# Which engine makes the second half of the weights' low parts in a two-block transformer kernel

## The reference, cut to what matters

```python
# block 1
h = rms_norm(x, norm_g)
dq, dk, dv, dg, mq, mk, mv, mg, gates = split(h @ w_in)
o_a = diff_attention(rope(dq), rope(dk), dv, lam) * silu(dg)     # 4 heads of 2 maps
o_b = moba_attention(rope(mq), rope(mk), mv) * silu(mg)          # 8 heads
merged = sigmoid(g_a) * (o_a @ w_branch_diff) + sigmoid(g_b) * (o_b @ w_branch_moba)
x = x + merged @ w_out            # then a gate: x + sigmoid(x @ w_ple_gate) * (p @ w_ple), final norm
# block 2
mod = silu(c) @ w_mod + b_mod     # six rows of 1024: shift, scale, gate, twice
h = rmsnorm(x) * (1 + sc1) + sh1
q, kc, vc, ks, vs, kw, vw, gates, cb, cc, ch = split(h @ w_in_2)
mixed = [norm(sparse_attention(...)), norm(cb * causal_conv(cc * ch))]
x = x + gt1 * (mixed @ w_out_2)
h2 = rmsnorm(x) * (1 + sc2) + sh2
q = h2 @ peer_wq                  # 16 experts of 128*128 per head and token by these keys
x = x + gt2 * sum_e gelu(h2 . u_e) * g_e * v_e                   # over all 16384 rows of u and v
```

## Time and profile before

| what | value |
|---|---|
| median of 3 runs | 1235.44 us (1234.71 to 1236.09) |
| the profiled execution's own time | 1233.38 us |
| its span, first to last instruction | 1231.6 us |
| busy in the span | PE 1191.4, DVE 910.5, ACT 782.5, POOL 565.2 us |
| PE clock granted, mean | 0.996 of full speed |

### The profile page before, as it was taken

One profiled execution on the slowest core, in us unless ns is written; L12 is line 12 of the kernel. 1 busy time (PEld: TensorE's weight loads), 2 busy tenths in 40 slices (PEclk: granted clock), 3 DMA queues, 4 the chain that ended last, 5 costly groups with the idle time before them and its releaser, 6 DMA issues.

```text
span 1231.6 us, 26652 instructions
## 1 busy us (share of the span) xinstructions
PE 1191.4 (97%) x8256; PEld 1070.6 (87%) x8256; DVE 910.5 (74%) x1885; ACT 782.5 (64%) x1784; POOL 565.2 (46%) x505
## 2 busy tenths in 40 slices
PE   8999999989998999999999999999999999999997
PEld 8888988988877999888999999998888888888886
DVE  5777768888577839996788888761676767686766
ACT  5446676465765555667877888876656555555555
POOL 3664543445464358998877777778100000000000
PEclk9999999999999999999999999999999999999999
DMA  6668655538643445655666666667676676767663
GB/s 233 227 212 296 235 193 202 172 121 290 249 140 120 137 138 179 185 185 170 214 212 197 204 213 201 210 209 266 203 245 212 189 258 189 260 197 257 191 196 108
DMA packets 85828, 249.86 MB, mean 203 GB/s; under 512 B 8019, under 2 KB 29692, under 8 KB 84988
## 3 DMA queue, kind: packets, MB, share of 16 engines
q1 hardware_dynamic: 77356, 209.62, 53.7%
q0 software_dynamic: 8400, 39.34, 8.7%
HBM read 237.38 MB, written 13.12 MB: 203 GB/s over the span
## 4 chain that ended last, share of the span: by engine, by line
PE 84%; DVE 6%; ACT 4%; issue 3%; POOL 3%; DVEq 0%; POOLq 0%; ACTq 0%
PE psum L695 83%; POOL w_lo L1645 2%; ACT w_hi L1218 1%; DVE w_lo L1815 1%; DVE s_sb L1829 1%; PE psum L896 1%; DVE arena L1868 1%; DVE rstd L1809 0%; ACT arena L1377 0%; ACT arena L1201 0%; DVE arena L2024 0%; DVE xres L1949 0%; DVE arena L1930 0%; ACT L1377 0%; DVE arena L2074 0%
## 5 line engine op out<-in xcount | busy, mean ns | idle before, releaser
L695 PE MATMUL psum<-h_parts,w_hi 128*128 128x256 f32 (+1 forms) x3216 | 676.3, 303 | 17.0 <-DVE h_parts L1859 4.4
L1645 POOL TENSOR_TENSOR w_lo<-ring,w_hi 128x512 fp32r<-128x512 f32 x368 | 490.7, 1344 | 273.3 <-ACT w_hi L1218 264.6
L1218 ACT ACTIVATE w_hi<-ring 128x512 fp32r<-128x512 f32 x734 | 445.2, 628 | 254.2 <-PE psum L695 243.7
L695 PEld LDWEIGHTS psum<-h_parts,w_hi 128*128 128x128 f32 x3216 | 515.5, 191 | 53.4 <-issue 21.2
L695 PE MATMUL psum<-h_parts,w_lo 128*128 128x256 f32 x1832 | 517.3, 282 | 0.0
L695 PEld LDWEIGHTS psum<-h_parts,w_lo 128*128 128x128 f32 x1832 | 350.1, 191 | 0.0
L695 PE MATMUL psum<-w_hi,h_parts 128*128 128x512 f32 (+1 forms) x1120 | 342.6, 388 | 3.8 <-DVE w_lo L1815 2.5
L695 PEld LDWEIGHTS psum<-w_hi,h_parts 128*128 128x128 f32 x1120 | 208.5, 188 | 48.9 <-issue 5.4
L1815 DVE TENSOR_TENSOR w_lo<-ring,w_hi 128x512 fp32r<-128x512 f32 x238 | 190.4, 800 | 77.7 <-ACT w_hi L1218 76.8
L695 PE MATMUL psum<-w_lo,h_parts 128*128 128x512 f32 (+1 forms) x560 | 216.2, 386 | 0.0
L2342 DVE TENSOR_TENSOR w_lo<-ring,w_hi 128x512 fp32r<-128x512 f32 x128 | 88.6, 692 | 62.0 <-ACT w_hi L1218 58.5
(11 more groups left out here) (214 smaller groups left out, 999.2 us busy)
## 6 DMA issues: line engine op xcount, KB each, us to landing
ring<-u_t SPq DMA_DIRECT2D x128, 512.0 KB, 3.6
ring<-v_rows SPq DMA_DIRECT2D x128, 512.0 KB, 3.6
ring<-weights SPq DMA_DIRECT2D x115, 512.0 KB, 4.0
arena<-mods POOLq DMA_DIRECT2D x48, 512.0 KB, 5.3
routing_weights<-s_sb SPq DMA_DIRECT2D x32, 320.0 KB, 4.1
s_sb<-routing_weights POOLq DMA_DIRECT2D x5, 2048.0 KB, 10.0
bias_rows<-bias_row POOLq DMA_DIRECT2D x1, 1536.0 KB, 11.3
xres<-x_t SPq DMA_DIRECT2D x2, 512.0 KB, 4.5
```

The lines of the kernel that those rows point to most:

```text
L695: return nc.tensor.matmul(out, lhs, rhs, start=start, stop=stop, **kw)
L1218: nc.scalar.activation(w_hi[:, half, :], src, ACT.Copy).then_inc(hi_done, 1)
L1645: nc.gpsimd.tensor_tensor(w_lo[:, half, :], src, w_hi[:, half, :].bitcast(F32), ALU.subtract)\
```

## The change

For every split slot from the third on, VectorE makes both halves of the low part: right behind half 0 it waits for the high part of half 1 and subtracts, and it counts `lo1_done` up. GpSimd keeps half 1 of slots 0 and 1, of slot ("proj", "nq1") and of slot 1 of "wq" (`NORM_SECOND`), and half 0 of slot 1. `FILLS` is empty, so the fillers are VectorE's too. Where the engine that makes half 1 changes from one slot to the next, the later engine waits until `lo1_done` has the earlier one's count. GpSimd waits for `lo1_done` at 111 before it starts on the tiles of `u`.

```diff
+FILLS = ()
+
+
+def pool_low(k):
+    s, i = SLOTS[SLOT_OF_SPLIT[k]]
+    return k < 2 or s[0] == "proj" and s[1] in FILLS or (s, i) in NORM_SECOND
+
+
+NORM_SECOND = ((("proj", "nq1"), 0), (("wq",), 1))
...
+            def second_half(k):
+                if pool_low(k):
+                    if k and not pool_low(k - 1):
+                        pool.wait_ge(lo1_done, k)
+                    src = ring[:, SLOT_OF_SPLIT[k] % RING, HSLOT:D]
+                    low(k, (2 * k + 1) % 4, src, 2 * k + 2, lo1_done)
...
-                    src = ring[:, SLOT_OF_SPLIT[k_lo] % RING, HSLOT:D]
-                    low(k_lo, (2 * k_lo + 1) % 4, src, 2 * k_lo + 2, lo1_done)
+                    second_half(k_lo)
                     k_lo += 1
...
+            pool.wait_ge(lo1_done, NSPLIT)
             low_tiles(0, POOL_TILES)
...
-            def low(half, src, hi_value):
+            def low(half, src, hi_value, done):
 
                 dve.wait_ge(hi_done, hi_value)
                 v.tensor_tensor(w_lo[:, half, :], src, w_hi[:, half, :].bitcast(F32), ALU.subtract)\
-                    .then_inc(lo0_done, 1)
+                    .then_inc(done, 1)
...
-                    low(2 * k_lo % 4, ring[:, SLOT_OF_SPLIT[k_lo] % RING, 0:HSLOT], 2 * k_lo + 1)
+                    slot = SLOT_OF_SPLIT[k_lo] % RING
+                    low(2 * k_lo % 4, ring[:, slot, 0:HSLOT], 2 * k_lo + 1, lo0_done)
+                    if not pool_low(k_lo):
+                        if pool_low(k_lo - 1):
+                            dve.wait_ge(lo1_done, k_lo)
+                        low((2 * k_lo + 1) % 4, ring[:, slot, HSLOT:D], 2 * k_lo + 2, lo1_done)
                     k_lo += 1
```

More of the change, by code:

```diff
@@ L2335, in low_act @@
                         .then_inc(act_lo, 1)
-                low(2 * (NSPLIT + P + s) % 4, ring[:, (NSLOT + P + s) % RING, 0:HSLOT], 2 * (NSPLIT + P + n) + 1)
+                low(2 * (NSPLIT + P + s) % 4, ring[:, (NSLOT + P + s) % RING, 0:HSLOT], 2 * (NSPLIT + P + n) + 1, lo0_done)
                 if final:
```

## The result

The changed kernel takes 1221.76 us in the median (1220.15 to 1224.54, 4 runs) beside 1235.08 (1233.89 to 1236.09, 4 runs), which is 13.3 us faster by the medians. The ratio of the two kernels is estimated at 0.9898, 95% interval 0.9886 to 0.9910, which is 12.6 us (11.1 to 14.1). The forecast was 1229.5 us with a range from 1223.5 to 1236: a gain of 5.9 us from the median that it started from. The direction was right, the size was less than half of what came, and the time lies outside the range. It is near that of the third rival (chance 0.15), whose 1223.2 us lies inside the spread of the four runs.

A forecast was written before the change was run, and what follows sets the result against it. TensorE, busy 97% of the span, was taken as the bound. Gains of 4.2 + 1.0 + 0.7 = 5.9 us took the profiled 1233.38 to 1227.5; 2.06 us for the median gave 1229.5 us, range 1223.5 to 1236.

The forecast's parts named there:

- third rival: Before 452 us: larger gain, all of 5.3, 1.7 and 1.2 us plus about 4 from unlisted holes; 1223.2 us, chance 0.15.
- What holds VectorE up: An operation with SBUF inputs beginning inside GpSimd's low part stands until that ends; one under way is not slowed.
- VectorE's account: Before 452 us: 107 added subtractions, 74.0 us, less 55.6 us of stalls; about 18 us busier of 123.7 idle.
- The stretch from 205 to 252: Merge and out1: VectorE's 41.2 us busy plus 11.1 added less 7.5 of stall gives 44.8 of 47 us.
- The wait for w_lo before dv: Before dv: TensorE's wanted low part begins at about 45.3 instead of 46.87, 1.5 us earlier; the 1.4 us wait goes.
- In the gate: Per gate slot, VectorE's two low parts and sum take 1.86 instead of 2.22 us; nothing won or lost, TensorE being full.
- The end of block 2's attention: Before TensorE's 3.6 us wait: about 1.2 us of GpSimd delay goes, reciprocal adds 0.5; net 0.7 us (-0.5 to 1.2).
- The modulation's wait: ScalarE's copy waiting 2.7 us for a modulation row, behind TensorE's 1.7 us wait: gain 1.0 us (0 to 1.7).
- its waits for low parts: TensorE's seven waits for VectorE's low parts before 452 us: 4.2 of 5.3 us gained, ends 0 and 5.3.
- the holes that no row names: Holes hidden by TensorE's busy time before 452 us: not in the forecast's sum; rival 3 gave them about 4 us.
- Rivals 1 and 2: 1: VectorE becomes bound in 205 to 252, 1238.7 us, chance 0.12. 2: waits move to next cause, 1233.9 us, chance 0.20.

The follow-up runs named there:

- the run with 1280 columns of zeros: Kernel before, half 1's low parts left out of the computation; GpSimd instead writes 1280 columns of zeros per slot, reading nothing: 1221.26 us beside 1234.28.
- the experiment above: Kernel before, but VectorE makes half 1 of two slots only, gate 0 and gate 1: 1233.48 us beside 1234.57, ratio 0.9992.
- the eights alone: Kernel before, but VectorE makes half 1 of the slots of merge, out1, gate, out2 and wq only (39 slots): 1231.60 us beside 1234.24.
- the out2 slot: Changed kernel, but GpSimd keeps half 1 of slot 2 of out2 as well: 1221.52 us, ratio to the kernel before 0.9900.

## Why the prediction was right in kind and wrong in size

- What holds VectorE up. Right in the main. A two-input operation with SBUF inputs that starts inside GpSimd's reading subtraction stands to about its end. That one under way is not slowed holds for most: two modulations that began first, by 0.36 us at 73.96 and by 0.03 at 82.20, took 2.75 and 2.40 us all the same, which no run here explains. The first of them, VectorE then GpSimd, in the kernel before:

```profile
73.96 2.75 DVE L1829 CUSTOM_DVE_ANT_0 s_sb<-arena,s_sb,par 128x1024 f32<-128x1024 f32 x1
```

```profile
74.32 1.30 POOL L1645 TENSOR_TENSOR w_lo<-ring,w_hi 128x512 fp32r<-128x512 f32 x1
```

  The Trainium skill (SBUF — State Buffer, Who interferes with whom) also says that a GpSimd operation that only writes does not do this; the run with 1280 columns of zeros agrees, 0.693 us against 0.927. The Trainium skill's page Perfetto Trace Analysis (Optimizing Scalar/DVE Operations) warns that shifting work between these two engines might not help; here the half that GpSimd had been given spared VectorE next to nothing (910.5 us busy with it, 911.3 without).
- VectorE's account. Predicted +74.0 us and -55.6, net +18; measured to 442 us: L1815 101.9 to 140.7, L1829 70.2 to 51.1, the two sums 15.2 to 4.5, net +9. The 74.0 was too much because a low part right behind another adds 0.60 us, not 0.69: 107 of them are 64. Smaller groups, which the prediction let cancel against stalls that stay, take nearly all of the rest off (L1949 6.9 to 3.8, L1840 11.9 to 9.6). The stretch from 205 to 252 was said to fit barely (44.8 of 47); its work takes 39.2 us of 45.8.
- The wait for w_lo before dv. Right to a few tenths: the low part was to begin at about 45.3 instead of 46.87.

```profile
44.70 0.43 DVE L1855 TENSOR_TENSOR arena<-arena 128x256 f32<-128x256 f32 x1
45.04 1.28 DVE L1830 TENSOR_TENSOR w_lo<-ring,w_hi 128x512 fp32r<-128x512 f32 x2
```

- In the gate two low parts and the sum take the place of one and a stalled sum (1.77 us by these rows, said 1.86), and nothing is won per slot:

```profile
255.59 1.29 DVE L1830 TENSOR_TENSOR w_lo<-ring,w_hi 128x512 fp32r<-128x512 f32 x2
256.80 0.48 DVE L1888 SCALAR_TENSOR_TENSOR arena<-arena,small 128x256 f32<-128x256 f32 x1
```

- The end of block 2's attention. ScalarE's square behind GpSimd waits 0.95 us instead of 1.88, and the reciprocal stands right behind the second low part, as said:

```profile
375.21 0.42 ACT L1213 ACTIVATE arena<-arena 128x256 f32<-128x256 f32 x1 [0.95 <-POOL arena L1768]
```

```profile
377.15 1.29 DVE L1830 TENSOR_TENSOR w_lo<-ring,w_hi 128x512 fp32r<-128x512 f32 x2 [2.65 <-ACT w_hi L1227]
378.36 1.75 DVE L1824 RECIPROCAL rstd<-std 128x256 f32<-128x256 f32 x1
```

  TensorE's longest wait fell from 3.6 to 2.9 us, the 0.7 of the sum. But a wait of 0.99 us for L1879 appeared behind it, so the group's total is 4.4 us as before, and at these two places TensorE lost 0.5 us instead of gaining 0.7.
- The modulation's wait, 1.0 us in the sum. Wrong: ScalarE waits 2.5 instead of 2.7 us, TensorE 1.6 instead of 1.7, and gains 0.2 us. Of what stood right before the modulation only one low part was stalled (1.74 us, at 191.19), and two low parts in 1.28 us took its place.
- The step that failed is the term "its waits for low parts: I take 4.2 of the 5.3 us, keeping 0 and 5.3 as ends", together with the holes that no row names, which the forecast put at nothing. The 3244 products of TensorE up to the tiles of `u` are the same and in the same order in both traces, so I took each distance from one product's start to the next in both and subtracted. The differences add up to the lead, 13.0 us, as they must; what they show is where it arises. Waits for low parts were worth 7.6 us, not 4.2, and 4.9 us come at 3209 places at which neither trace lists a wait. The other places with a listed wait give 0.6 us together, with the 0.2 and the -0.5 of the last two bullets in it.
- Why the first part was missed: 3.0 us in 3 waits stood under the name of w_hi. They are 1.0 at mv (84 us), where the low part stood behind a modulation of 2.40 us, 1.5 at the gate, where it was stalled itself (the experiment above), and 0.4 at out2. I had read that row and put it down to ScalarE, as its name says. The gate's is shown to be a wait for w_lo. At mv the product starts at 85.47, 0.26 us behind its low part (84.53 + 0.68) as well, and the wait is gone in the runs that hand mv over. At out2 a wait of 0.4 us for w_lo stands in its place after the change; whose it was before is not shown. The rows of w_lo and w_hi together fell from 8.3 to 1.5 us.
- Why the second was missed: TensorE's busy time is modelled, and the view of waits lists only what is left of a hole beyond it. 18 places gained more than 0.1 us each without a listed wait, 3.3 us together; the rest is smaller still. Rival 3 named such holes and gave them 4 us. That its time came out is in part luck: its other terms, 1.7 and 1.2 us for the modulation and the end of the attention, brought -0.3 us together, and 2.2 us of waits booked on ScalarE, which it did not have, made up for most of that. Nor could the 9% of the chain on VectorE and GpSimd, its evidence, tell the size: after the change these two hold 14% of the chain.
- Rivals 1 and 2. The first is refuted for the change (the eights alone are 2.6 us faster). With GpSimd's reading kept, VectorE does become too full, but mostly elsewhere than in the stretch that this rival named. The second, waits that move on to the next cause, holds for the end of the attention and for the out2 slot.

What stays open: which of the many small holes belong to which stalled instruction, and the two modulations that were held up although they began first.

## What to carry to other kernels

Before work goes from GpSimd to VectorE or back, price GpSimd's instruction by what it holds up on VectorE as well as by its own time: here 107 subtractions of 1.3 us cost VectorE about as much by stalls as doing them itself costs (L1815's group grew by 39 us, all of VectorE by next to nothing). The profile books a wait on the last of several releasers; if another beside it is stalled, keep both as candidates until a small experiment on that place decides. And where TensorE's busy time is modelled, compare the starts of its products one by one, since the places with a listed wait held only 8.2 of the 13.0 us.

## What the runs showed of the hardware that was not expected

GpSimd's writing into SBUF for 1.37 us a slot (0.53 + 0.53 + 0.31) beside VectorE's two-input float32 subtraction costs the latter nothing (0.693 us, 110 of them), while GpSimd's reading subtraction of 1.23 us, even of a constant tile, makes them 0.26 us longer in the mean. Two low parts behind each other on VectorE start 0.60 us apart (1.29 us for two), so the second costs less than the 0.69 us of its row.

The hold goes both ways. In the kernel before, the modulation on VectorE began first here and took its normal time, and GpSimd's low part, begun 0.27 us later, took 2.13 us instead of 1.29:

```profile
189.99 1.28 DVE L1829 CUSTOM_DVE_ANT_0 s_sb<-arena,s_sb,par 128x1024 f32<-128x1024 f32 x1
```

```profile
190.26 2.13 POOL L1645 TENSOR_TENSOR w_lo<-ring,w_hi 128x512 fp32r<-128x512 f32 x1 [3.93 <-ACT w_hi L1218]
```

37 of GpSimd's 112 low parts took over 1.35 us, 10.6 us more than 1.29 each in all.
